# Attention of a two-block transformer: transposes grouped by pair of heads, the low half's subtraction on GpSimd, and DMA issues on SyncE

## The reference

```
scores = einsum(q, k) * dh**-0.5 + bias;  scores = where(mask, scores, -1e30)
p = softmax(scores);  o = einsum(p, v)              # neighbourhood, 8 heads
s = einsum(q, k) * dh**-0.5;  p = softmax(s)
o = einsum(p, v);  y = o @ w_o                      # second block, 16 heads
```

## Time and profile before

| | |
|---|---|
| three runs, median (lowest to highest) | 3004.83 us (3002.92 to 3008.61) |
| the profiled execution, its own time | 3003.72 us |
| its span in the profile | 3001.9 us |
| busy in the span: PE, DVE, ACT, POOL | 2674.1, 1563.1, 1084.3, 1051.6 us |
| PE busy in the two stretches with attention | 302.93 of 352 us, 357.17 of 413 us |

### The profile page before, as it was taken

One profiled execution on the slowest core, in us unless ns is written; L12 is line 12 of the kernel. 1 busy time (PEld: TensorE's weight loads), 2 busy tenths in 40 slices (PEclk: granted clock), 3 DMA queues, 4 the chain that ended last, 5 costly groups with the idle time before them and its releaser, 6 DMA issues. The chain is left out here.

```text
span 3001.9 us, 37777 instructions
## 1 busy us (share of the span) xinstructions
PE 2674.1 (89%) x14592; PEld 2169.9 (72%) x14592; DVE 1563.1 (52%) x2351; ACT 1084.3 (36%) x1959; POOL 1051.6 (35%) x510
## 2 busy tenths in 40 slices
PE   1788889899999889888699999997799999699998
PEld 1666567678887666656488888886787888488886
DVE  2544426654544445555665655555567686622223
ACT  2354343332222454444421121114456555422222
POOL 2225324534444411111223333333344444344443
PEclk9999899999999899999899999998899999799999
DMA  5544214333333000000133333321111111022221
GB/s 195 185 160 149 78 53 140 130 133 133 127 134 126 29 22 19 19 18 18 50 124 115 113 127 120 120 99 47 50 50 50 50 50 60 25 92 94 96 99 71
DMA packets 80547, 267.74 MB, mean 89 GB/s; under 512 B 8560, under 2 KB 14320, under 8 KB 80368
## 3 DMA queue, kind: packets, MB, share of 16 engines
q1 hardware_dynamic: 70416, 248.67, 24.0%
q10 hardware_dynamic: 9664, 15.34, 1.6%
q0 software_dynamic: 288, 1.31, 0.1%
HBM read 260.57 MB, written 4.72 MB: 88 GB/s over the span
## 5 line engine op out<-in xcount | busy, mean ns | idle before, releaser
L1979 POOL TENSOR_TENSOR SLO<-RAW,SHI 128x1024 fp32r<-128x1024 f32 (+1 forms) x336 | 815.9, 2430 | 1628.1 <-ACT SHI L1809 1628.1
L1809 ACT ACTIVATE SHI<-RAW 128x1024 fp32r<-128x1024 f32 (+1 forms) x336 | 346.2, 1033 | 1117.6 <-PE PS L2238 1084.2
L2236 PE MATMUL PS<-HLh,SHI 128*128 128x512 f32 x1680 | 688.8, 410 | 30.9 <-DVE HLl L2044 19.0
L2237 PE MATMUL PS<-HLl,SHI 128*128 128x512 f32 x1680 | 661.2, 394 | 0.0
L2238 PE MATMUL PS<-HLh,SLO 128*128 128x512 f32 x1680 | 660.9, 393 | 0.0
L2236 PEld LDWEIGHTS PS<-HLh,SHI 128*128 128x128 f32 x1680 | 319.7, 190 | 127.3 <-issue 47.2
L2236 PE MATMUL PS<-hh,SHI 128*128 128x512 f32 (+1 forms) x944 | 356.0, 377 | 16.8 <-DVE hl L2128 9.9
L2238 PEld LDWEIGHTS PS<-HLh,SLO 128*128 128x128 f32 x1680 | 318.9, 190 | 69.3
L2237 PEld LDWEIGHTS PS<-HLl,SHI 128*128 128x128 f32 x1680 | 320.6, 191 | 64.2 <-issue 6.3
L2237 PE MATMUL PS<-hl,SHI 128*128 128x512 f32 (+1 forms) x944 | 347.8, 368 | 0.0
L2238 PE MATMUL PS<-hh,SLO 128*128 128x512 f32 (+1 forms) x944 | 347.7, 368 | 0.0
(11 more groups left out here) (233 smaller groups left out, 3894.0 us busy)
## 6 DMA issues: line engine op xcount, KB each, us to landing
RAW<-in_k_w SPq DMA_DIRECT2D x316, 512.0 KB, 3.2
ADA<-in_k_w SPq DMA_DIRECT2D x132, 512.0 KB, 4.0
early<-in_k_w SPq DMA_DIRECT2D x12, 512.0 KB, 10.6
RAW<-in_k_w SPq DMA_DIRECT2D x20, 256.0 KB, 2.6
XL<-in_xT ACTq DMA_DIRECT2D x1, 2048.0 KB, 12.6
bi<-in_k_bias ACTq DMA_DIRECT2D x16, 128.0 KB, 3.0
out<-XL SPq DMA_DIRECT2D x8, 256.0 KB, 2.1
bi<-in_k_bias ACTq DMA_DIRECT2D x8, 192.0 KB, 3.6
```

The costliest lines, as they stand in the source:

```text
L1809: eng.activation(u.hi, u.w, ACT.Copy).then_inc(S["a_hi"], 1)
L1979: eng.tensor_tensor(u.lo, u.w, u.hi.bitcast(F32), ALU.subtract).then_inc(S["g_lo"], 1)
L2236: eng.matmul(st.out, lh, rh, start=st.first and j == 0, stop=False)
L2237: eng.matmul(st.out, lh, rl, start=False, stop=False)
```

## The change

- `s2` now takes a pair. Its blocks (both items') stand in one row; four fill a bank where the buffer pt holds both items (256 and 384 keys in the first block, all in the second), else three (dilated). The second block's pt is now 2 buffers of 1536 columns and not 3 of 768. The first of these transposes stands ahead of `s3`, all others behind it. `s2` yields after each.
- `normed` writes its product to o in SBUF, of which there are now two, and gives the bank back after DVE's product. `out_split` reads o; the low half is made by POOL.
- hh and hl of the second block's attention are two buffers, not three: the scores of tile i wait in the plan for `out2(i-2)`, where they waited for `out2(i-3)`.
- the biases, and the trips of the values to HBM and back, are issued by SP, in the place that the plan gives them among the loads of weights.

```
-        def s2(it):
-            e, t_e = st[id(it)]
-            nk = it["n"] // 128
-            p = W["pt"].next()
-            toks = []
-            for j0 in range(0, nk, 3):
-                j1 = min(nk, j0 + 3)
+        def s2(pair):
+            es, t_es = zip(*(st[id(it)] for it in pair))
+            nk = pair[0]["n"] // 128
+            wide = W["pt"].peek().ap.shape[1] >= 2 * pair[0]["n"]
+            cells = [W["pt"].next()] * 2 if wide else [W["pt"].next(), W["pt"].next()]
+            at = (0, nk) if wide else (0, 0)
+            blocks = [(h, j) for h in range(2) for j in range(nk)]
+            step = 4 if wide else 3
+            for n0 in range(0, 2 * nk, step):
+                part = blocks[n0:n0 + step]
...
         def normed(b, t_mm):
             o = W["o"].next()
             t_rb, t = tick("a_rb"), tick("v_onorm")
-            put(OutNorm(b.ap, o.ap, b.ap[:, 256:384], t_mm, o.free, t_rb, t))
-            o.free = [t]
-            return b, t
+            put(OutNorm(b.ap, o.ap, t_mm, o.free, t_rb, t))
+            give(b, t)
+            return o, t
...
-            if turn:
-                s2(pairs[i - 2][0])
+            turns = s2(pairs[i - 2]) if turn else iter(())
+            for _ in turns:
                 yield
+                break
             if read:
                 done = normed(*s3(pairs[i - 3]))
                 yield
-            if turn:
-                s2(pairs[i - 2][1])
-                yield
+            yield from turns
...
-    def out_split(bank, t_o, src, hi, lo, t_free):
-        t1, t2 = tick("a_ohi"), tick("v_olo")
+    def out_split(o, t_o, src, hi, lo, t_free):
+        t1, t2 = tick("a_ohi"), tick("g_olo")
         put(OutSplit(src, hi, lo, t_o, t_free, t1, t2))
-        give(bank, t2)
+        o.free = [t1, t2]
...
-        heads += marked(att_items(i, hid[i % 3]), [f"q2 {i}"] + [f"out2 {i - 3}"] * (i > 2), f"att {i}")
+        heads += marked(att_items(i, hid[i % 2]), [f"q2 {i}"] + [f"out2 {i - 2}"] * (i > 1), f"att {i}")
...
-    vn_read.append(dma("act", vscr.rearrange("(t p) n -> p t n", p=128), vn, vn_tok))
+    vn_read.append(dma("sp", vscr.rearrange("(t p) n -> p t n", p=128), vn, vn_tok))
...
-            biases[n] = (c.ap[:, 0:wide[1]], dma("act", c.ap[:, 0:wide[1]],
+            biases[n] = (c.ap[:, 0:wide[1]], dma("sp", c.ap[:, 0:wide[1]],
...
-        return sorted(adas + units, key=lambda u: u.at)
+        own = [(i, st) for i, st in enumerate(plan) if type(st) is Dma and st.queue == "sp"]
+        return sorted([(u.at, u) for u in adas + units] + own[1:], key=lambda p: p[0])
```

More of the change, by code:

```diff
@@ L742, in s2 @@
                 on = "a" if flip[0] else "v"
-                work[0] += 128 * 2 * (j1 - j0)
+                work[0] += 256 * len(part)
                 t_mm, t2 = tick("p_flip"), tick(on + "_flip")
-                put(Flip(e.ap, nk, j0, j1, b.ap, p.ap, on, t_e, b.free, t_mm, p.free, t2))
+                p, (h0, j0) = cells[hs[0]], part[0]
+                dst = p.ap[:, 128 * (at[h0] + j0):128 * (at[h0] + j0 + len(part))]
+                put(Flip([es[h].ap[:, 128 * j:128 * j + 128] for h, j in part], b.ap, dst, on, [t_es[h] for h in hs],
+                         b.free, t_mm, p.free, t2))
                 give(b, t2)
-                toks.append(t2)
-            e.free = [t_mm]
-            st[id(it)] = (p, toks)
+                for h in hs:
+                    toks[h].append(t2)
+                    es[h].free = [t_mm]
+                yield
+            for h, it in enumerate(pair):
+                st[id(it)] = (cells[h], at[h], toks[h])
         def shares(it):
@@ L761, in s3 @@
         def s3(pair):
-            ps, toks = zip(*(st.pop(id(it)) for it in pair))
+            ps, at, toks = zip(*(st.pop(id(it)) for it in pair))
             ds = [dgs.pop(id(it)) for it in pair]
@@ L1381, in build_program @@
         if i > 0:
-            dense += [after(f"att {i - 1} done"), out2(i - 1, hid[(i - 1) % 3]), note(f"out2 {i - 1}")]
+            dense += [after(f"att {i - 1} done"), out2(i - 1, hid[(i - 1) % 2]), note(f"out2 {i - 1}")]
     weave((attention(heads, W, make2), 1.25), (pipelined(dense), 1.0))
     st, stc = Stats(NT, W), Stats(NC, W)
-    run(out2(7, hid[7 % 3], [st, stc]))
+    run(out2(7, hid[7 % 2], [st, stc]))
     claim(True)
@@ L1776, in _ @@
             sp = Waiter(eng, S)
-            own = [st for st in steps if isinstance(st, Dma) and st.queue == "sp"]
-            for st in own[:1]:
-                eng.dma_start(st.dst, st.src).then_inc(S[st.name], 16)
-            for u in load_order():
-                sp.wait_ge(u.t_free)
-                src = t_in["k_w"][u.off:u.off + 128 * u.sz].rearrange("(p n) -> p n", p=128)
-                eng.dma_start(u.buf, src).then_inc(S[u.raw], 16)
-            for st in own[1:]:
-                sp.wait_ge(st.waits)
-                eng.dma_start(st.dst, st.src).then_inc(S[st.name], 16)
+            eng.dma_start(plan[0].dst, plan[0].src).then_inc(S[plan[0].name], 16)
+            for _, x in load_order():
+                if type(x) is Dma:
+                    sp.wait_ge(x.waits)
+                    eng.dma_start(x.dst, x.src).then_inc(S[x.name], 16)
+                else:
+                    sp.wait_ge(x.t_free)
+                    src = t_in["k_w"][x.off:x.off + 128 * x.sz].rearrange("(p n) -> p n", p=128)
+                    eng.dma_start(x.buf, src).then_inc(S[x.raw], 16)
             for n in dma_names:
@@ L1849, in flip_ @@
                     a.wait_ge(st.t_mm, st.t_pfree)
-                    n = 128 * (st.j1 - st.j0)
-                    eng.activation(st.p[:, 128 * st.j0:128 * st.j1], st.bank[:, 0:n], ACT.Copy).then_inc(S["a_flip"], 1)
+                    eng.activation(st.p, st.bank[:, 0:128 * len(st.blocks)], ACT.Copy).then_inc(S["a_flip"], 1)
             def share(st):
@@ L2261, in flip_ @@
                 p.wait_ge(st.t_exp, st.t_bank)
-                for j in range(st.j0, st.j1):
-                    i = eng.transpose(st.bank[:, 128 * (j - st.j0):128 * (j - st.j0) + 128],
-                                      st.e[:, 128 * j:128 * j + 128], ident)
+                for j, e in enumerate(st.blocks):
+                    i = eng.transpose(st.bank[:, 128 * j:128 * j + 128], e, ident)
                 i.then_inc(S["p_flip"], 1)
```

51 lines of the change are left out of this document (26 added, 25 removed).

## The result

| | median (lowest to highest) | |
|---|---|---|
| the kernel before | 3003.89 us (3002.92 to 3008.61), 4 runs | |
| the changed kernel | 2931.37 us (2930.45 to 2934.08), 4 runs | ratio 0.9757, 95% interval 0.9740 to 0.9774 |

A forecast was written before the change was run, and what follows sets the result against it. PE was taken to set the time (busy 2674.1 of 3001.9 us), with gains only where it idles or runs at its lower clock. Second block -18 and first block -7 made -25: 3004.8 to 2980 us, range 2955 to 3002.

The forecast's parts named there:

- Order at the norms: Second block's attention: product placed between a norm's sum and its bank's next user shortens PE's waits, -8 us (0 to -14).
- Banks and DVE's stop: Second block's attention: output bank returns after DVE's product and DVE stops no more for the high half, -5 us.
- Fewer copies: Second block's attention: four blocks to a bank give 112 copies for 160, -3 us (0 to -6).
- GpSimd's subtraction: Second block's attention: low half on POOL at 0.5 us, uncovered before output projections of 8 tiles, +2 us (0 to +4).
- Two output buffers: Second block's attention: tile 7's scores wait for `out2(5)`, leaving pairs near the end without dense work, +4 us (0 to +8).
- Clock: Second block's attention: three and a half of about nine falls to the lower clock go, -8 us (+5 to -15).
- First block: First block's attention: DMAs moved to SP, fewer copies, earlier bank, free DVE and POOL's subtractions, -7 us (+5 to -14).
- the DMAs: First block's attention: ACT freed of the DMAs at 99.43 us shortens PE's wait for the square, -4 us (+3 to -6).
- a bias that lands late stops DVE: First block's attention: risk of biases queued on SP behind write and weight load, 1 us taken back for it.
- more than thought: Rival: DVE's stops behind most residual waits, all clock falls but two go, -10 and -14 us more, 2957 us; chance 0.09.
- Gaps only move: Rival: waits for the four banks reappear one step later and the clock falls as often, 2998 us; chance 0.16.
- Slower by the clock at rows of transposes: Rival: rows of transposes count as idle for the clock, half of 32 wide pairs bring falls, 3025 us; chance 0.06.

The follow-up runs named there:

- b_out: Kernel before with the output's product in SBUF, bank given back after the product, low half on GpSimd: ratio 0.9850, -45 us.
- c_step3: Kernel before with transposes in the change's order, two output buffers and pt of 1536, but three blocks to a bank: ratio 0.9946, -16 us.
- e_mid: Kernel before with output in SBUF and low half on GpSimd, but bank given back after ACT's high half: ratio 0.9904, -29 us.
- c_dve: Kernel before with output in SBUF and bank given back after the product, but low half left on DVE: ratio 1.0011, +3 us.
- a_mix: Changed kernel with HBM writes and biases on ACT, only the reads back on SP: ratio 0.9734 to the kernel before, -80 us.

## Why the prediction was right or wrong

*Order at the norms, forecast -8.* The size is right, its cause only in part. ACT r, DVE f and POOL q ended 19.8 us of PE's idle time and end 9.4 now. From the third tile on it is the 1.2 us that I worked out (0.49 + 0.69); in the first two places 1.33 and 2.64 us, where I kept 2.8. But I gave all of it to the order, and the order alone leaves 20.9 us under these names; the two output buffers, to which I gave a price of +4, have a part in it.

*Banks and DVE's stop, forecast -5, bounds 0 to -10.* This is the step that failed. I took only the waits that named a residual (DVE XL) and gave a third of them, and I let no wait under another name and no fall of the clock hang on this part. The part run alone (b_out) gives 45 us, 37 of them in the second stretch. There the waits for DVE XL fall from 14.4 us to 3.8, those for ACT pt from 10.9 to 5.5 and those for DVE's low half from 3.2 to 0; in all 18.5 us of idle time go, and 27.3 us less at the lower clock are 14 more. The timelines show a way from the stop to ACT's copies: the stop delays the maximum, the maximum ACT's exponential, and that the copy behind it. ACT r (12.5 and 12.0) and POOL q (4.1 and 5.1) don't fall with it. Of the 45 us the runs put 29 on taking the low half off DVE and 16 on the early bank beside it (both stretches, kernel before).

*Fewer copies, forecast -3.* Mis-sized by most, in the same way. I argued from the engines' time, which "hardly moves", and gave the 48 banks a third of the 10 us that named a copy. The fourth block is worth 29 us with the stop in place, and the split copies show that it isn't the engines' time. What it is worth beside the output's part was not run.

*GpSimd's subtraction, forecast +2.* The estimate of 0.5 us was near (0.459), and at the output projections PE waits 2.3 us for it where it waited 1.5 for DVE's.

*Two output buffers, forecast +4.* The bare stretch is there as the order showed it, but its three waits are 0.53, 0.67 and 0.59 us (1346 to 1354 us), where I had 1.45 a pair from the last pair of before. Alone the step gave -11: it also moves the dense work against the pairs. POOL q goes from PE's waits (4.1 us) and ACT r falls from 12.5 to 8.7, while ACT pt rises from 10.9 to 16.8. Why that helps by so much was not tested; beside the grouping it is +3 within the intervals.

*Clock, forecast -8.* 30.7 us less at the lower level are 15 us. I tied the falls to the places at the norms, and the trace's record of the granted clock bears that out: of the eight falls in the second stretch before, six start at a tile's norm (1082, 1117, 1171, 1229, 1287 and 1345 us) and a seventh at the wait for the rotated queries behind one (1403). The change has none of the seven, and one at the end of the stretch (1380 us); I had counted on three and a half. Nor do they go with the sum of the waits: c_step3 has 48.0 us idle and 10.2 at the lower level, e_mid 42.5 and 20.5. Single waits don't decide it either: two falls of c_step3 (1170 and 1221 us) stand at a wait of 2.5 us, and the change keeps one of 2.64 without a fall. What decides stays open. The remaining 8 us of shorter busy time aren't explained by the clock: c_step3 and b_out both have 10.2 us at the lower level in the second stretch, and 345.5 and 336.0 us of busy PE. The one with more waits has more busy time. What a restart after a short wait adds to "busy" was not measured by itself.

*First block, forecast -7, measured -19.5 in the stretch.* For the DMAs I gave -4, with "a bias that lands late stops DVE" as the risk. The risk came true, by way of the modulation weight in the same queue: 5.6 us. I had taken four to five us for the write to land, as on ACT's queue; on SP's, behind a weight load, it was 9.6. The 15 us that came beside them are those of the output's part alone in this stretch, for which I had carried over a share of the second block's small sum.

Of the rivals, *more than thought* (2957, 0.09) came nearest: nearly all waits for residuals went, and all but one fall in the second stretch. It was still 26 us short, since it left the fourth block at 3 and the first block at 7; its own terms add up to 2956. *Gaps only move* was wrong: the second sum's wait is 0.49 us. *Slower by the clock at rows of transposes* was wrong: in the changed kernel the window from 1200 to 1220 us, which holds 22 transposes in groups of four and one of eight, has PE busy 19.95 of 20 us at the higher level all through:

```profile
1200.00:1220.00 20.00, 19.95 (x154) 14.73 (x153) 11.13 (x25) 10.72 (x29) 2.89 (x5) 1.00 0.08 27
```

The Trainium skill's rule that transposes don't count as busy (TensorE: Matmul & The Clock Gate, Part 4: PE-mode transpose) has no effect at such lengths here.

What held the sum down was one way of reading: I priced each step by the waits that bore its name. The names tell who came last. Much of the time at the lower clock and of the idle time hung on the same two things, a bank more or less and a DVE that stands: the parts that touch these give 45 us each, the others 0 to 3 beside them.

## What to carry to other kernels

Where a few banks are passed round in turn and every engine works in order, price a step that frees a bank or ends an engine's stop by the whole chain behind it (here the maximum, the exponential, the copy), not by the waits that name it: 29 us for taking a stop off DVE where the waits that named its residuals had 14, and 29 us for three tenths fewer banks of transposes, 24 of them kept with more engine time. Steps of this kind overlap: 45 and 45 gave 73. Before a piece is called worth nothing, look at each stretch: the +3 of c_dve was -10 in one and +9 in the other, where moving an operand to SBUF had doubled DVE's subtraction. When DMAs move to the queue of the weights, keep those that a wait follows apart from those that anything urgent stands behind: the write on one queue and its reads on the other gave the 7 us that moving all of them did not.

## What the hardware showed that I had not expected

A write of 1 MB to HBM took 4.6 us to land when ACT's queue issued it at 99.43 us (5.0 in a_mix), and 9.6 us when SP's issued it 0.44 us behind a weight load of 0.5 MB. The load of the mask by GpSimd's queue (0.75 MB) also went out 0.5 us ahead of it then, and 1.4 us behind it in the other two; the two causes weren't separated. A subtraction of 128x128 on DVE took 0.291 us with an operand in PSUM and 0.400 with both in SBUF; GpSimd took 0.459. Where the result is written with a stride (first block, neighbourhood attention), DVE took 0.382 us with an operand in PSUM and 0.785 with both in SBUF, GpSimd 0.648. Copies of 256 and 512 columns out of PSUM took 0.418 and 0.684 us on DVE, 0.38 and 0.594 on ACT.
